# Hybrid encoder trunk: where the squares of the last tile are summed, and two pieces of ScalarE work moved

## The chip, the core and the metric

The kernel runs on one core of a Trainium2 chip. The metric is the device time of one execution in microseconds (us), the median of several runs; a profile is one such execution with the hardware profiler on. The engines are TensorE (PE; its weight loads are shown apart as PEld), VectorE (DVE), ScalarE (ACT), GpSimd (POOL) and SyncE (SP), which issues most loads.

## The reference

Two layers over 512 tokens of 1024 channels. `rms` divides each token by the root of its mean square and multiplies by a gain.

```python
for l in range(2):
    h = (silu(rms(x) @ w_gate) * (rms(x) @ w_up)) @ w_out      # 1024 -> 2 x 2816 -> 1024
    x = x + 0.5 * rms(h)
    h = rms(x) @ mix_w_in                                      # DeltaNet heads | convolution channels
    o = concat(gated_delta_rule(h), silu(layer_norm(causal_conv31(glu(h)))))
    x = x + rms(o @ mix_w_out)
    h = (silu(rms(x) @ w_gate2) * (rms(x) @ w_up2)) @ w_out2
    x = rms(x + 0.5 * rms(h))
```

In the gated delta rule the tokens are in chunks (the kernel takes four of 128), a state is carried from chunk to chunk, and the output `o` of each head is divided by the root of its mean square.

## The kernel before

Channels lie on the partitions (8 tiles of 128 for `x`), tokens on the free axis. Each large product is made of three products of rounded parts: high weight by high input, high by low, low by high (`tile`, lines 656 to 660). ScalarE makes the high part of a weight slot (`high`, line 1365), VectorE the low part (`weight_low`, line 2099). The engines run in parallel, each through its own instructions in the order in which they are written, and are held together by semaphores that count; nothing plans the order but this text.

**Stages and hand-overs.** Each layer has an FFN, a mixer and an FFN. Behind each stage but the very last, its output `y` (8 tiles) is normalised and added to `x`, and the next stage's inputs `xh` and `xl` are made: a hand-over, five in all (three behind an FFN, two behind a mixer). For this the sum of `y`'s squares over all channels is needed. ScalarE squares each tile from its bank into `sqr` (`y_square`); VectorE adds tiles 0 to 6 into `acc` (`y_sum`, line 2109, semaphore `ysum`). The last tile is made in two token halves of 256. When the first half is done (`y_half`), ScalarE squares it (line 1385, `ylast_sq`), VectorE adds it to `acc` (`y_sum_half`, line 2168, `ysum_part`), and TensorE sums over the channels with products by a column of ones (`token_sums`, line 665: one per chunk of 128 tokens, each shown as two records). ScalarE takes the root (line 1388), VectorE the reciprocal, TensorE spreads it over the partitions (`spread_first`, line 689), VectorE updates `x` (lines 2149, 2150), ScalarE makes `xh` (line 1406), VectorE `xl` (line 2160), and TensorE starts the next stage with half the tokens of three input tiles (lines 748, 750, 755). Meanwhile TensorE makes the second half of the last tile: in an FFN the last 8 of 22 steps (`k0` to `k0 + 7`), in the mixer 8 steps (`mix_last`). The second half's squares go the same way inside the next stage's first products, in `next_inputs` on VectorE and in `y_second_sums` on TensorE.

**First Strassen pairs.** The 16 middle gate/up pairs of each of the four FFNs are Strassen forms (`body`). ScalarE makes from a gate weight a negated copy (line 1503), to which GpSimd's accumulating DMA adds the weight (line 606, `form_added`), and the high part (line 1504), twice, one half at a time. In the first body ScalarE does the silu of the last plain pair (`silu(SP0 - 1, 0)`, line 1487) and then `first_forms(1, 0)`. VectorE waits for this silu in `pair(4, ...)` and goes on with the form sums (lines 2288 to 2290), the low parts (2314, 2298) and `up_second` (line 2321), which raises `c22_out`. TensorE's product `p4` of the pair before waits for `c22_out` (line 903); it is the third of the products of the second body.

**The scan.** For each of four chunks `c` ScalarE scales the state (line 1935), copies the new values `vn` (line 1938) and the keys (line 1924), and squares the chunk's output (`o_square(c)`, line 1905), which waits for `on` from VectorE (line 2773). TensorE's products that read `vn` are at lines 1256 and 1260, those that give it at line 1241.

Of the kernel before, what the change touches and what calls it, by code (L numbers as in the profile page):

```python
# [19 lines left out]
ALU = mybir.AluOpType  # L20
# [26 lines left out]
def trunk_kernel(nc, x, ffn1_norm_pre, ffn1_w_in, ffn1_w_out, ffn1_norm_post, mix_norm_pre, mix_w_in,  # L47
# [11 lines left out]
    KD = D // P  # L59
# [195 lines left out]
    with ctx:  # L255
# [28 lines left out]
        def sem(name):  # L284
# [21 lines left out]
        ylast_sq = sem("ylast_sq")  # L306
        y_half, ysum_part, ssq_part, root_part, col_part, bc_part, x_part, xh_part, xs_part = [
            sem(n) for n in ("y_half", "ysum_part", "ssq_part", "root_part", "col_part", "bc_part", "x_part",
                             "xh_part", "xs_part")]
# [310 lines left out]
        def _(pe):  # L620
# [50 lines left out]
            def x_sums(stage, l):  # L671
# [4 lines left out]
                else:  # L676
                    token_sums(acc[:]).then_inc(ssq_full, 1)

            def y_first_sums(stage, l):
                pe.wait_ge(ysum_part, (3 * l + stage) * 2 + 1)  # L680
                token_sums(acc[:], chunks=HALVES[0]).then_inc(ssq_part, 1)

            def y_second_sums(hand):
                pe.wait_ge(ysum_part, hand * 2 + 2)
                token_sums(acc[:], chunks=HALVES[1]).then_inc(ssq_full, 1)

# [32 lines left out]
            def first_units(u0, stage, stat_q, l):  # L719
# [40 lines left out]
                if stage or l:  # L760
                    for n in range(3):
                        pe.wait_ge(lo_full, l * UNITS + (u0 + n + 1 + SLOTS))
                    for k in range(HALVED):
                        pe.wait_ge(xh_part, hand * HALVED + k + 1)
                        high_products(k, tokens_of(0))
                        if k == 1:
                            spread_second(before, bl)
                        pe.wait_ge(xs_part, hand * HALVED + k + 1)
                        low_products(k, tokens_of(0))
                        if k == 0:  # L770
                            y_second_sums(hand)
                    for k in range(KD):
                        tokens = tokens_of(1) if k < HALVED else slice(0, T)
                        pe.wait_ge(xh_ready, l * NXS + stage * KD + k + 1)
                        high_products(k, tokens)
                        pe.wait_ge(xs_ready, l * NXS + stage * KD + k + 1)
                        low_products(k, tokens)
# [96 lines left out]
            def ffn(f, l):  # L874
# [80 lines left out]
                for m in range(KD):  # L955
                    pe.wait_ge(y_done, l * NY + (m + YB + stage * KD - 3))
                    for part, (k0, nk) in enumerate(OUT_PARTS):
# [8 lines left out]
                        for k in range(k0, k0 + nk):  # L966
# [4 lines left out]
                            if m < KD - 1:  # L971
                                mm = tile(in_bank(y_bank(m, stage, l)), n % SLOTS, k - k0, hh[:, k, :], hl[:, k, :],
                                          k == 0, k == KF - 1)
                            else:
                                mm = half_tile(k, 0)
                                if part < 2:
                                    mm = half_tile(k, 1)
                        if m == KD - 1 and part == 2:
                            mm.then_inc(y_half, 1)
                            for k in range(k0, k0 + nk):  # L980
                                if k == k0 + 3:
                                    y_first_sums(stage, l)
                                if k == k0 + 5:
                                    spread_first(stage, l)
                                mm = half_tile(k, 1)
                        mm.then_inc(unit_done, 1)

            for l in range(L):
# [309 lines left out]
                def mix_last(part):  # L1298
                    tokens = tokens_of(part)
                    for k in range(2 * CT):  # L1300
                        if part and k == 3:
                            y_first_sums(1, l)
# [57 lines left out]
        def _(act):  # L1360
# [93 lines left out]
            def ffn(f, l):  # L1454
# [104 lines left out]
                def body(s, odd, first=False, final=False, plain=None):  # L1559
# [3 lines left out]
                    first_part(s, odd)  # L1563
                    if first:
                        silu(SP0 - 1, 0)
                    if final:
                        act.wait_ge(prod_done, st * PRODS + 7 * s + 2)
                        high(u0 + 2 * (KF - 1), 2, 8, l)
                    else:
                        first_forms(s + 1, 1 - odd)  # L1570
                    if plain is not None and not odd:
                        act.wait_ge(conv_lo, plain + (st * NCONV + 1))
# [151 lines left out]
            for l in range(L):  # L1724
# [203 lines left out]
                for c in range(NC):  # L1928
# [12 lines left out]
                    if c == NC - 2:  # L1941
                        keys_out(c + 1)
                    if c == 0:
                        z_refill(0)
# [5 lines left out]
                    if c == 3:  # L1950
                        z_gate(1)

                        act.activation(warm[:], eps[:], ACT.Sqrt)
                    o_square(c)
                act.wait_ge(oss_ready, l * (H + 1) + H + 1)
# [95 lines left out]
        def _(dve):  # L2051
# [111 lines left out]

            def y_sum_half(part, stage, l):
                dve.wait_ge(ylast_sq, (3 * l + stage) * 2 + part + 1)
                dve.wait_ge(ysum, l * NYQ + (stage + 1) * (KD - 2))
                tokens = tokens_of(part)
                dve.tensor_tensor(acc[:, tokens], acc[:, tokens], sqr[:, (KD - 1) % 2, tokens],
                                  ALU.add).then_inc(ysum_part, 1)

            def row_first(stage, l):
                y_sum_half(0, stage, l)
                dve.wait_ge(root_part, 3 * l + stage + 1)
# [6 lines left out]
            def next_inputs(stage, gain, l):  # L2180
# [4 lines left out]
                low_half(0, 0, stage, gain, l)  # L2185
                y_sum_half(1, before, bl)
                update_half(2, 0, before, bl)
# [761 lines left out]
```

## Time and profile before

| | us |
|---|---|
| median of 3 runs (lowest, highest) | 1975.64 (1975.39, 1976.35) |
| the profiled execution | 1976.71 |
| its span | 1975.0 |

| engine | busy us | share of the span |
|---|---|---|
| PE | 1946.8 | 99% |
| PEld | 1746.6 | 88% |
| DVE | 1430.2 | 72% |
| ACT | 1161.8 | 59% |
| POOL | 149.4 | 8% |

TensorE's granted clock was 0.999 of full speed over the span. An engine's idle time counts only if another engine or the end waits for what comes behind it.

### The profile page before, as it was taken

What the parts mean: (1) busy time and instruction counts of PE and PEld (TensorE: products, weight loads), DVE (VectorE), ACT (ScalarE), POOL (GpSimd) and SP (SyncE); (2) the same over time, 40 slices, a digit from 0 to 9 for tenths busy, and PEclk for the clock granted to TensorE, in tenths of its full rate; (3) what the DMA queues carried; (4) which work ended last, traced back from release to release, by engine and by line L of the source; (5) the groups of instructions that cost most, each with busy time, mean ns of one, the idle gap of its engine ahead of it and who ended that gap; (6) DMA issues with size and microseconds to landing.
All of it is one profiled execution on the core that took longest, in us unless ns stands there. A gap on an engine that the chain in (4) does not pass through costs nothing.

```text
span 1975.0 us, 33173 instructions
## 1 busy us (share of the span) xinstructions
PE 1946.8 (99%) x12162; PEld 1746.6 (88%) x12162; DVE 1430.2 (72%) x2109; ACT 1161.8 (59%) x1957; POOL 149.4 (8%) x196
## 2 busy tenths in 40 slices
PE   9999999999999999999999999999999999999997
PEld 7999988878988899988889999888889888999886
DVE  5889832699885888872388888337998868888524
ACT  6576742457866667662266767325587656676513
POOL 1111000011000011100001110000110000111000
PEclk9999999999999999999999999999999999999999
DMA  6466533276222366643326664432761224666421
GB/s 177 116 153 155 144 110 102 68 170 147 65 54 86 86 150 159 156 127 96 102 65 138 156 155 121 116 103 75 171 141 45 61 78 114 153 158 148 150 96 43
DMA packets 351426, 232.52 MB, mean 118 GB/s; under 512 B 11122, under 2 KB 324948, under 8 KB 351316
## 3 DMA queue, kind: packets, MB, share of 16 engines
q1 hardware_dynamic: 327396, 177.55, 31.5%
q0 software_dynamic: 23904, 53.49, 15.0%
q8 instruction: 70, 1.15, 0.2%
q14 instruction: 40, 0.33, 0.0%
q10 hardware_dynamic: 16, 0.00, 0.0%
HBM read 175.43 MB, written 2.10 MB: 90 GB/s over the span
## 4 chain that ended last, share of the span: by engine, by line
PE 78%; DVE 15%; ACT 3%; issue 2%; DMA 1%; SPq 0%; POOL 0%; DVEq 0%; ACTq 0%
PE res L658 10%; PE res L660 9%; PE res L659 9%; PE res L893 8%; PE res L896 7%; PE res L895 7%; DVE u L2522 6%; PE sp L824 3%; PE sp L896 3%; PE sp L895 3%; PE sp L893 3%; PE res L824 2%; DVE cacc L2604 2%; PE sp L658 1%; PE res L755 1%
## 5 line engine op out<-in xcount | busy, mean ns | idle before, releaser
L2099 DVE TENSOR_TENSOR wl<-raw,wh 128x1024 fp32r<-128x1024 f32 (+1 forms) x167 | 197.3, 1185 | 335.2 <-ACT wh L1365 334.6
L1365 ACT ACTIVATE wh<-raw 128x1024 fp32r<-128x1024 f32 (+1 forms) x205 | 209.7, 1029 | 329.5 <-PE res L660 235.9
L893 PE MATMUL res<-xh,wh 128*128 128x256 f32 x768 | 218.1, 284 | 3.3 <-ACT wh L1523 1.7
L895 PE MATMUL res<-xl,wh 128*128 128x256 f32 x768 | 217.3, 283 | 0.0
L896 PE MATMUL res<-xh,wl 128*128 128x256 f32 x768 | 217.3, 283 | 0.0
L658 PE MATMUL res<-xh,wh 128*128 128x512 f32 x536 | 213.5, 398 | 2.1 <-DVE xl L2217 1.8
L660 PE MATMUL res<-xh,wl 128*128 128x512 f32 x536 | 208.9, 390 | 0.0
L659 PE MATMUL res<-xl,wh 128*128 128x512 f32 x536 | 208.9, 390 | 0.0
L660 PE MATMUL res<-hh,wl 128*128 128x512 f32 (+1 forms) x528 | 198.4, 376 | 0.0
L659 PE MATMUL res<-hl,wh 128*128 128x512 f32 (+1 forms) x528 | 198.4, 376 | 0.0
L658 PE MATMUL res<-hh,wh 128*128 128x512 f32 (+1 forms) x528 | 198.4, 376 | 0.0
L606 POOL DMA_DIRECT2D wl<-raw x128 | 109.0, 856 | 985.2 <-ACT wl L1503 972.7
L2522 DVE SCALAR_TENSOR_TENSOR u<-glu,call,u 128x512 f32<-128x512 f32 x240 | 167.8, 745 | 0.3
L893 PEld LDWEIGHTS res<-xh,wh 128*128 128x128 f32 x768 | 147.3, 192 | 4.9 <-ACT wh L1523 2.7
L895 PEld LDWEIGHTS res<-xl,wh 128*128 128x128 f32 x768 | 147.4, 192 | 0.2
L896 PEld LDWEIGHTS res<-xh,wl 128*128 128x128 f32 x768 | 147.4, 192 | 0.0
L893 PE MATMUL res<-th,wh 128*128 128x256 f32 x512 | 145.0, 283 | 1.3 <-ACT us L1542 1.3
L895 PE MATMUL res<-tl,wh 128*128 128x256 f32 x512 | 144.9, 283 | 0.0
L895 PE MATMUL sp<-tl,wh 128*128 128x256 f32 x512 | 144.9, 283 | 0.0
L896 PE MATMUL sp<-th,wl 128*128 128x256 f32 x512 | 144.9, 283 | 0.0
L893 PE MATMUL sp<-th,wh 128*128 128x256 f32 x512 | 144.9, 283 | 0.0
L896 PE MATMUL res<-th,wl 128*128 128x256 f32 x512 | 144.9, 283 | 0.0
(421 smaller groups left out, 4891.3 us busy)
## 6 DMA issues: line engine op xcount, KB each, us to landing
raw<-in_ffn_w_in SPq DMA_DIRECT2D x176, 512.0 KB, 4.0
wl<-raw POOLq DMA_DIRECT2D x128, 256.0 KB, 5.3
raw<-in_mix_w_in SPq DMA_DIRECT2D x48, 512.0 KB, 3.9
raw<-in_ffn_w_out SPq DMA_DIRECT2D x46, 512.0 KB, 3.9
raw<-in_ffn_w_out SPq DMA_DIRECT2D x48, 448.0 KB, 3.8
wl<-raw POOLq DMA_DIRECT2D x38, 512.0 KB, 4.6
raw<-in_mix_w_out SPq DMA_DIRECT2D x16, 512.0 KB, 4.0
xin<-in_x SPq DMA_DIRECT2D x8, 256.0 KB, 5.0
```

Of the source, the lines that this page charges most:

```text
L606: pool.dma_start(wl[:, 2, ks, :].bitcast(F32), raw[:, 2 * ((SP0 + s) % 2), ks, :], accum_op=ALU.add).then_inc(form_added[half], 16)
L658: pe.matmul(bank, wh[:, slot, j, :], hi, start=first, stop=False)
L659: pe.matmul(bank, wh[:, slot, j, :], lo, start=False, stop=False)
L660: return pe.matmul(bank, wl[:, slot, j, :], hi, start=False, stop=last)
L824: mm = pe.matmul(row_banks(c)[:, half, :], h[:, k, tokens], w[:, k % SLOTS, 4 * half:4 * half + 4, :].rearrange("p a b -> p (a b)"), start ...
L893: pe.matmul(bank, wh[:, slot, j, :], hi[:, k, :], start=first and k == 0, stop=False, skip_group_check=True)
L895: pe.matmul(bank, wh[:, slot, j, :], lo[:, k, :], start=False, stop=False, skip_group_check=True)
L896: mm = pe.matmul(bank, wl[:, slot, j, :], hi[:, k, :], start=False, stop=k == 3, skip_group_check=True)
L1365: act.activation(wh[:, slot, 0:nk, :], raw[:, slot, 0:nk, :], ACT.Copy).then_inc(hi_full, 1)
L2099: dve.tensor_tensor(wl[:, slot, 0:nk, :], raw[:, slot, 0:nk, :], wh[:, slot, 0:nk, :].bitcast(F32), ALU.subtract).then_inc(lo_full, 1)
L2522: ins = dve.scalar_tensor_tensor(u[:, t, :], src, w, u[:, t, :], ALU.mult, ALU.add)
L2604: ins = dve.scalar_tensor_tensor(cacc[:, n % 2, :], pre[:, k:k + T], w, cacc[:, n % 2, :], ALU.mult, ALU.add)
```

## The change

The first halves' and second halves' additions on VectorE (`y_sum_half`) are gone. TensorE sums `acc` (tiles 0 to 6, all four chunks) on its own in `y_other_sums` and then adds the last tile's squares straight from `sqr` into the same column sums. `y_other_sums` stands before step `k0 + 2` of the first half in an FFN and before step 6 in the mixer; the first half's sums stand one step earlier than before; the second half's stand between the high and the low products of input tile 0. `spread_first` and `spread_second` stay where they were. The silu in the first Strassen body follows `first_forms`. `o_square(c)` follows the copies of chunk `c + 1`, and the last stands behind the loop.

```diff
--- before.py
+++ after.py
@@ -304,8 +304,8 @@
         gate_scaled, pair_free, silu_done, h_ready = sem("gate_scaled"), sem("pair_free"), sem("silu_done"), sem("h_ready")
         y_done = sem("y_done")
         ylast_sq = sem("ylast_sq")
-        y_half, ysum_part, ssq_part, root_part, col_part, bc_part, x_part, xh_part, xs_part = [
-            sem(n) for n in ("y_half", "ysum_part", "ssq_part", "root_part", "col_part", "bc_part", "x_part",
+        y_half, ssq_part, root_part, col_part, bc_part, x_part, xh_part, xs_part = [
+            sem(n) for n in ("y_half", "ssq_part", "root_part", "col_part", "bc_part", "x_part",
                              "xh_part", "xs_part")]
         dve_step, pair_step = sem("dve_step"), sem("pair_step")
         mix_free = sem("mix_free")
@@ -676,13 +676,17 @@
                 else:
                     token_sums(acc[:]).then_inc(ssq_full, 1)
 
+            def y_other_sums(stage, l):
+                pe.wait_ge(ysum, l * NYQ + (stage + 1) * (KD - 2))
+                token_sums(acc[:], last=False)
+
             def y_first_sums(stage, l):
-                pe.wait_ge(ysum_part, (3 * l + stage) * 2 + 1)
-                token_sums(acc[:], chunks=HALVES[0]).then_inc(ssq_part, 1)
+                pe.wait_ge(ylast_sq, (3 * l + stage) * 2 + 1)
+                token_sums(sqr[:, (KD - 1) % 2, :], first=False, chunks=HALVES[0]).then_inc(ssq_part, 1)
 
             def y_second_sums(hand):
-                pe.wait_ge(ysum_part, hand * 2 + 2)
-                token_sums(acc[:], chunks=HALVES[1]).then_inc(ssq_full, 1)
+                pe.wait_ge(ylast_sq, hand * 2 + 2)
+                token_sums(sqr[:, (KD - 1) % 2, :], first=False, chunks=HALVES[1]).then_inc(ssq_full, 1)
 
             def spread_half(part):
                 for n, c in enumerate(HALVES[part]):
@@ -763,12 +767,12 @@
                     for k in range(HALVED):
                         pe.wait_ge(xh_part, hand * HALVED + k + 1)
                         high_products(k, tokens_of(0))
+                        if k == 0:
+                            y_second_sums(hand)
                         if k == 1:
                             spread_second(before, bl)
                         pe.wait_ge(xs_part, hand * HALVED + k + 1)
                         low_products(k, tokens_of(0))
-                        if k == 0:
-                            y_second_sums(hand)
                     for k in range(KD):
                         tokens = tokens_of(1) if k < HALVED else slice(0, T)
                         pe.wait_ge(xh_ready, l * NXS + stage * KD + k + 1)
@@ -972,13 +976,15 @@
                                 mm = tile(in_bank(y_bank(m, stage, l)), n % SLOTS, k - k0, hh[:, k, :], hl[:, k, :],
                                           k == 0, k == KF - 1)
                             else:
+                                if part == 2 and k == k0 + 2:
+                                    y_other_sums(stage, l)
                                 mm = half_tile(k, 0)
                                 if part < 2:
                                     mm = half_tile(k, 1)
                         if m == KD - 1 and part == 2:
                             mm.then_inc(y_half, 1)
                             for k in range(k0, k0 + nk):
-                                if k == k0 + 3:
+                                if k == k0 + 2:
                                     y_first_sums(stage, l)
                                 if k == k0 + 5:
                                     spread_first(stage, l)
@@ -1298,7 +1304,9 @@
                 def mix_last(part):
                     tokens = tokens_of(part)
                     for k in range(2 * CT):
-                        if part and k == 3:
+                        if not part and k == 6:
+                            y_other_sums(1, l)
+                        if part and k == 2:
                             y_first_sums(1, l)
                         if part and k == 5:
                             spread_first(1, l)
@@ -1561,13 +1569,13 @@
                     first_sum(s, odd, first)
                     act.sem_inc(hi_full, 2)
                     first_part(s, odd)
-                    if first:
-                        silu(SP0 - 1, 0)
                     if final:
                         act.wait_ge(prod_done, st * PRODS + 7 * s + 2)
                         high(u0 + 2 * (KF - 1), 2, 8, l)
                     else:
                         first_forms(s + 1, 1 - odd)
+                    if first:
+                        silu(SP0 - 1, 0)
                     if plain is not None and not odd:
                         act.wait_ge(conv_lo, plain + (st * NCONV + 1))
                     second_part(s, odd)
@@ -1940,6 +1948,8 @@
                         keys_out(c + 1)
                     if c == NC - 2:
                         keys_out(c + 1)
+                    if c:
+                        o_square(c - 1)
                     if c == 0:
                         z_refill(0)
                         act.wait_ge(o_full, l * NC + 1)
@@ -1951,7 +1961,7 @@
                         z_gate(1)
 
                         act.activation(warm[:], eps[:], ACT.Sqrt)
-                    o_square(c)
+                o_square(NC - 1)
                 act.wait_ge(oss_ready, l * (H + 1) + H + 1)
                 act.activation(gt["orr"][:, 0:16], gt["oss"][:, 16:32], ACT.Sqrt).then_inc(oroot, 1)
                 z_refill(2)
@@ -2161,15 +2171,7 @@
                                          xh[:, k, tokens].bitcast(F32), ALU.mult,
                                          ALU.subtract).then_inc(xs_ready if part else xs_part, 1)
 
-            def y_sum_half(part, stage, l):
-                dve.wait_ge(ylast_sq, (3 * l + stage) * 2 + part + 1)
-                dve.wait_ge(ysum, l * NYQ + (stage + 1) * (KD - 2))
-                tokens = tokens_of(part)
-                dve.tensor_tensor(acc[:, tokens], acc[:, tokens], sqr[:, (KD - 1) % 2, tokens],
-                                  ALU.add).then_inc(ysum_part, 1)
-
             def row_first(stage, l):
-                y_sum_half(0, stage, l)
                 dve.wait_ge(root_part, 3 * l + stage + 1)
                 dve.reciprocal(rcol[:, 0:2], rsq[:, 0:2]).then_inc(col_part, 1)
 
@@ -2183,7 +2185,6 @@
                 update_half(0, 0, before, bl)
                 update_half(1, 0, before, bl)
                 low_half(0, 0, stage, gain, l)
-                y_sum_half(1, before, bl)
                 update_half(2, 0, before, bl)
                 row_second(before, bl)
                 low_half(1, 0, stage, gain, l)
```

## Rows read from the trace of the kernel before

**Rows 1.** TensorE's waits: who was waited for, us in total, times, longest.

```profile
PE res L748 <- ACT xh L1406: 4.4, 10, 0.6
...
PE res L755 <- DVE xl L2160: 1.9, 5, 0.4
PE sp L1256 <- ACT vn L1938: 1.8, 2, 1.0
...
PE res L893 <- ACT wh L1523: 1.7, 2, 1.1
PE res L893 <- ACT us L1542: 1.3, 1, 1.3
PE res L893 <- ACT wh L1513: 1.1, 2, 0.6
```

**Rows 2.** Timeline of the first hand-over: start, length, engine, line, tiles, [idle before].

```profile
364.88 0.38 PE L689 MATMUL sp<-ident,rcol 128*128 128x128 f32 x2
...
367.54 0.28 PE L750 MATMUL res<-xh,wl 128*128 128x256 f32 x1
...
368.02 0.50 PE L665 MATMUL sp<-ones,acc 128*128 128x1 f32 x4
...
371.48 0.39 PE L748 MATMUL res<-xh,wh 128*128 128x256 f32 x1 [0.33 <-ACT xh L1406]
```

**Rows 3.** Timeline of TensorE around four chunks of token sums.

```profile
36.59 0.94 PE L665 MATMUL sp<-ones,acc 128*128 128x1 f32 x8
37.39 0.49 PE L658 MATMUL sp<-xh,wh 128*128 128x512 f32 x1
```

**Rows 4.** Timeline of the first mixer's last tile, first half: steps 0 and 6.

```profile
624.84 0.28 PE L658 MATMUL res<-hig,wh 128*128 128x256 f32 x1
...
627.00 0.28 PE L658 MATMUL res<-hic,wh 128*128 128x256 f32 x1
...
627.34 0.69 DVE L2109 TENSOR_TENSOR acc<-acc,sqr 128x512 f32<-128x512 f32 x1
```

**Rows 5.** Timeline of VectorE before the first hand-over: tile 6 of an FFN.

```profile
352.06 0.68 DVE L2109 TENSOR_TENSOR acc<-acc,sqr 128x512 f32<-128x512 f32 x1
```

**Rows 6.** Timelines of VectorE, TensorE and ScalarE in the first layer's scan.

```profile
560.00 0.68 DVE L2764 TENSOR_TENSOR St<-sd,sp 128x512 f32<-128x512 f32 x1
...
563.46 1.06 PE L1241 MATMUL sp<-St,Wy 128*128 128x128 f32 x8
...
564.02 0.31 ACT L1905 ACTIVATE osq<-on 128x128 f32<-128x128 f32 x1 [7.20 <-DVE on L2773]
...
567.00 1.16 PE L1256 MATMUL sp<-vn,kdec 128*128 128x128 f32 x8 [0.90 <-ACT vn L1938]
...
577.13 0.31 ACT L1905 ACTIVATE osq<-on 128x128 f32<-128x128 f32 x1 [0.89 <-DVE on L2773]
```

**Rows 7.** Timelines around the first Strassen pair of FFNs 1, 2 and 3.

```profile
78.91 0.41 DVE L2321 TENSOR_TENSOR us<-us,res 128x256 f32<-128x256 f32 x1
...
81.81 0.28 PE L893 MATMUL sp<-th,wh 128*128 128x256 f32 x1
...
693.20 0.63 ACT L1487 ACTIVATE gs<-gs 128x512 f32<-128x512 f32 x1 [0.37 <-DVE gs L2250]
...
695.30 0.61 ACT L1504 ACTIVATE wh<-raw 128x512 fp32r<-128x512 f32 x1
...
699.52 0.42 DVE L2321 TENSOR_TENSOR us<-us,res 128x256 f32<-128x256 f32 x1
...
701.15 0.28 PE L893 MATMUL sp<-th,wh 128*128 128x256 f32 x1
...
1050.96 0.63 ACT L1487 ACTIVATE gs<-gs 128x512 f32<-128x512 f32 x1 [2.09 <-DVE gs L2250]
...
1057.29 0.41 DVE L2321 TENSOR_TENSOR us<-us,res 128x256 f32<-128x256 f32 x1
...
1058.88 0.28 PE L893 MATMUL sp<-th,wh 128*128 128x256 f32 x1
```

## The prediction

> **What bounds the kernel now.** I read the table of busy times (above) first: TensorE is busy for 99% of the span, so the time is TensorE's instruction stream plus the few places where it waits. Then I read TensorE's list of waits [rows 1]. The reader is to see that the waits which this change can touch are small and counted: ten of 0.44 us on the first products of a stage (two at each of five hand-overs), two of 0.9 us in the scan on `vn`, and in the four FFNs single waits on what the first Strassen pairs need: 1.7 us in two, 1.3 in one, 1.1 in two. Then I read a hand-over in order of time [rows 2], the price of sums on TensorE [rows 3], the mixer's and the FFN's last tiles [rows 4, 5], the scan [rows 6] and the first Strassen pairs [rows 7]. What is added to TensorE's stream counts in full, and so does a wait that goes. Outside these places it does not wait for ScalarE or VectorE, so a shift there changes nothing.
>
> **The sums of squares, and where they cost.** A 256-column product follows the one before it in 0.12 us: the 18 products from 624.84 to 627.00 take 2.16 us [rows 4]. Four chunks of token sums are eight records, and the product behind them starts 0.80 us after their first [rows 3]; that product then takes 0.49 us instead of 0.39, 0.1 us for the start behind them. I take 0.88 us for four chunks. Two chunks are the x4 record group at 368.02 [rows 2]. Before, each hand-over had four chunks (two and two). After, it has eight: `y_other_sums` sums the accumulated squares alone, and the two halves of the last tile are summed as before, straight from `sqr`. So 0.88 us is added at each of 5 hand-overs, 4.4 us.
> These eight records stand in front of the product that raises `y_half`, so nothing hides them: everything behind `y_half` starts later by as much.
> The Trainium skill's page "TensorE: Matmul & The Clock Gate", section "Back-to-back issue gap", gives an isolated product N/2.4 + 2.5 ns, some 3 ns for a product of one column; by that the four chunks would cost nothing and the sum of this change would be 4.4 us lower. The same section says that in a stream the spacing is set by the weight load too. The row gives 0.10 us for each of the eight records, so it decides for the second statement.
>
> **The wait that comes with it.** `y_other_sums` needs the sum over tiles 0 to 6. In an FFN VectorE has done it early: tile 6's is at 352.06 [rows 5], some 8 us ahead of the place. In the mixer the last tile has only 8 steps a half, and the sums are put before step 6, which TensorE reaches at 627.00, while VectorE's last addition starts at 627.34 and takes 0.69 [rows 4], done at 628.03. TensorE stands in order, so its products wait 1.05 us. VectorE can't be earlier: the addition is behind a weight subtraction that waits for ScalarE. This is paid in 2 mixers: 2.1 us. Behind the waiting sums stand the last six products of the half, `y_half`, the Square, the root and the whole hand-over.
>
> **What the removed additions give.** First half: the sums of the squares may start when the Square is done, about 0.45 us sooner, and are moved from behind three steps to behind two (0.36 us). But `spread_first` stays before step 5, and TensorE reaches it at 364.88 in either order, having done the same sums and the same steps. VectorE and ScalarE have nothing else to do for the result. I take 0; at most it is the 0.36 us by which the sums move.
> Second half: the sums move ahead of the three low products, from 368.02 to 367.66 (0.12 behind the last high product at 367.54) [rows 2]. The root, the scaling of the last tile and `xh` of tile 2, which stand in order on ScalarE, move 0.36 us, and VectorE, rid of its addition (0.42 us), follows. TensorE's wait at 371.48 (0.33 us, with the slower start behind it) goes, and from there VectorE's additions and subtractions set the pace for two more steps, all 0.36 us earlier. So 0.36 us is won at each of 5: 1.8 us. The bounds are 0 and the two waits together, 0.33 and one of 0.4 on `xl`.
> Sum of this part: 4.4 + 2.1 - 1.8 = **+4.7 us**. TensorE does more, and the chain that was shortened was not the one that decided.
>
> **The scan's squares.** In iteration 2 ScalarE is held at `o_square(1)` for 7.20 us until VectorE gives `on` at 564.02, and has its four squares (0.31 us each, some 1.2 together), four scalings and the copy of `vn` still to do. What these need is there earlier: the state at 560.68 and TensorE's values at 564.52 [rows 6]. Squares last, `vn` is ready at about 565.1, and TensorE, which stood 0.90 us before 567.00, doesn't wait. The slower start behind a wait goes too (1.16 instead of 1.06 us). 1.0 us. VectorE's state update waits for the same products and moves along. What is late next is the last square: `o_square(3)` at 577.13 [rows 6] is now behind `o_square(2)`, a silu and a table load. ScalarE gets there at about 576.4, so it wins 0.75 where TensorE wins 1.0; the row of roots and the first turned head lie behind it and are nearly tight, which costs 0.15. I take -0.85 us a layer, **-1.7 us**, between 0 and -2.0.
>
> **The silu behind the second pair's weights.** The silu and the four copies behind it start 0.52 us apart: silu at 693.20, the fourth copy at 695.30 [rows 7]. With the silu last, ScalarE hands the first copy to the accumulating DMA 0.5 us earlier (and by its own idle wait for VectorE more), and TensorE's wait for this DMA shrinks. But the silu itself starts some 2 us later, and behind it VectorE is stuck in order: the product `hraw`, three form sums, two weight subtractions, then `up_second`, for which the product p4 of the first pair waits (`c22_out`). This gives four sums, in the order of the FFNs:
> First: `up_second` starts at 78.91, +2.0 and 0.41 long, done at 81.3; p4 stood at 81.81 and could be at 81.3 with its DMA wait 0.5 shorter: -0.4.
> Second: the silu waited 0.37 for `gs`, so it is 1.7 late; `up_second`, at 699.52 before, + 1.7 + 0.42 and 0.05 of signalling gives 701.7, while p4 was at 701.15: +0.55 and 0.08 of slower start, +0.6.
> Third: the silu waited 2.09 us for `gs` (1050.96) and held up the copies behind it, and thereby the copy that TensorE waited for (1.3 us in rows 1). It still runs at 1050.96, so VectorE loses nothing; p4 goes from 1058.88 to the end of `up_second`, 1057.29 + 0.41 and signalling: -1.05.
> Fourth: like the second, but it had a DMA wait of 0.56 us to lose: about +0.1.
> Sum -0.75, **-0.7 us**. Bounds: all of the four waits won, -3.1; the second's loss in each, +2.4.
>
> **The sum.** The profiled execution took 1976.71 us, its span 1975.0. With 4.7 - 1.7 - 0.7 = +2.3 us it is 1979.0. The median shown is 1.07 us lower, so the change gives 1977.9 against 1975.64. About 0.2% (4 us) is what can be told from no change.
>
> **Rivals.**
> (A) The late silu costs nothing, because p4 does not really wait for `up_second` or VectorE catches up. Then the four waits go whole, -3.1 instead of -0.7: 1975.5. For it: VectorE has idle time after `up_second` in the first pairs. Against: its row ends only 1.2 us before p4 in the second FFN.
> (B) The added records hide behind the running products: -4.4, 1973.5. Against it stands the row of eight.
> (C) Slower: ScalarE and not TensorE ends the scan. The moved `o_square(2)`, the silu and the table load stand before `o_square(3)`; if `vn` of chunk 3 comes less than 0.8 us earlier, the last root, the scaling of `on` and the first turned head are no earlier than before, or 0.3 later. It takes the whole 1.7 and 0.3 in each layer: +2.3, 1980.2, slower by 0.23%. It decides from the point where those 1.2 us of squares are more than ScalarE won.
>
> **Chances.** Forecast 0.62, A 0.15, B 0.06, C 0.13, others 0.04. The likeliest one's own range is 1976.5 to 1979.3; with A and C and the bounds of the silu the range is 1974.6 to 1980.2. Faster by over 0.2% (below 1971.7) needs B and A together: 0.03. Slower by over 0.2% (above 1979.6) is most of C and the upper edge of the forecast: 0.14. Same 0.83.
>
> **What would show it.** TensorE's busy time up by some 4 us. In both mixers a wait of about 1 us of the sums on VectorE's addition to `acc`, in no FFN. At the hand-overs the first wait on `xh` unchanged at 0.54, the second gone or small. No wait on `vn`. In the second and fourth FFN a new wait, at p4 of the first pair, on VectorE's `us`; the third's 1.3 us gone. I would be wrong if the mixers show no wait on `acc`, if the first wait on `xh` shrinks too, or if p4 starts without one.

## The result, and the profile after

| | before | after |
|---|---|---|
| median of 5 runs (lowest, highest) | 1975.64 (1975.17, 1976.98) | 1984.59 (1982.18, 1987.12) |
| profiled execution, its span | 1976.71, 1975.0 | 1982.39, 1980.7 |
| mean granted clock of the profiled execution | 0.999 | 0.997 |

The changed kernel is slower by 0.43%: the ratio is 1.0043, with the interval 1.0032 to 1.0054. I had said 1977.9 and a range up to 1980.2; it is 6.7 us above the one and 4.4 above the other.

TensorE's list of waits in the changed kernel, to be held against [rows 1] (who was waited for: us in total, times, longest):

```profile
PE res L897 <- DMA wl<-raw: 4.4, 5, 1.5
PE res L752 <- ACT xh L1414: 2.8, 5, 0.6
...
PE sp L665 <- DVE acc L2119: 1.8, 2, 0.9
...
PE sp L897 <- DVE us L2322: 0.6, 1, 0.6
...
PE sp L665 <- DVE usum L2743: 0.3, 1, 0.3
```

Three lines are as forecast. The waits on `xh` are 5 and not 10. The wait on `acc` is there, twice, 0.92 us each. The one on `vn` (1.8 us) is gone. The first line is the surprise: 4.4 us of waits on the accumulating DMA, where [rows 1] has 4.1 us on ScalarE's `wh` and `us` (and the kernel before one of 0.5 us on this DMA).

Three timelines of the changed kernel (start, length, engine, line, tiles, [idle before]). First TensorE at the first hand-over, to be held against [rows 2]:

```profile
366.19 0.36 PE L752 MATMUL res<-xh,wh 128*128 128x256 f32 x1 [0.54 <-ACT xh L1414]
...
366.98 0.50 PE L665 MATMUL sp<-ones,sqr 128*128 128x1 f32 x4
367.34 0.60 PE L759 MATMUL res<-xl,wh 128*128 128x256 f32 x3
...
370.45 0.39 PE L752 MATMUL res<-xh,wh 128*128 128x256 f32 x1
```

The first wait keeps its 0.54 us. The second sums stand ahead of the three low products, and the 0.33 us in front of the product that was at 371.48 have gone. Then the first mixer, against [rows 4]:

```profile
625.09 0.28 PE L660 MATMUL res<-hic,wl 128*128 128x256 f32 x1
626.29 1.05 PE L665 MATMUL sp<-ones,acc 128*128 128x1 f32 x8 [0.92 <-DVE acc L2119]
627.21 0.36 PE L658 MATMUL res<-hic,wh 128*128 128x256 f32 x1
...
625.55 0.68 DVE L2119 TENSOR_TENSOR acc<-acc,sqr 128x512 f32<-128x512 f32 x1
```

From the last product to the next one are 2.12 us where there were 0.12: the wait, the eight records, and the start behind them. And the scan, against [rows 6]:

```profile
563.44 0.60 ACT L1946 ACTIVATE vn<-sp 128x512 f32<-128x512 f32 x1 [2.47 <-PE sp L1247]
...
564.41 0.31 ACT L1913 ACTIVATE osq<-on 128x128 f32<-128x128 f32 x1
...
564.83 1.05 PE L1262 MATMUL sp<-vn,kdec 128*128 128x128 f32 x8
...
575.36 0.31 ACT L1913 ACTIVATE osq<-on 128x128 f32<-128x128 f32 x1 [0.23 <-DVE on L2774]
```

ScalarE makes `vn` before the four squares, and TensorE's products on it start without a wait.

**Where the 5.7 us of span went.** I matched TensorE's instructions of the two traces one by one and took the shift between them in front of and behind each place; a step is the difference, with the slower start behind a wait in it:

| place | predicted | in the trace |
|---|---|---|
| three hand-overs behind an FFN | 3 x 0.52 | 3 x 0.42 (+0.79, then -0.37) |
| two behind a mixer | 2 x 1.57 | 1.71 each, and 1.3 more in layer 2 |
| scan, both layers | -1.7 | -0.70 and -1.10 |
| first Strassen pairs, FFN 1 to 4 | -0.4, +0.6, -1.05, +0.1 | 0, +0.67, -0.18, +0.15 |
| later Strassen pairs | 0 | +1.2 (-0.7 at 222, +1.0 at 728, +0.4 at 1078, -0.6 at 1190, +1.15 at 1818) |
| start of the kernel | 0 | -0.7 |
| behind TensorE's last product, and drift | 0 | +0.3 |

Two of these are not the change's doing. The start is 0.7 us earlier in this execution and not at all in a second one of the same kernel (number 10). And of the step at 1190, some 0.8 us stand at 1197, where ten of the eleven profiles taken after the kernel before gain 0.45 to 0.8 us on its profile, whatever the edit.

The 1.3 us more in layer 2 stand in the granted clock. Stretches of the changed kernel (busy us of PE, PEld, DVE, ACT, POOL with counts, then the clock, the DMA share and GB/s):

```profile
1604.00:1608.00 4.00, 3.08 (x26) 2.88 (x26) 1.83 (x2) 1.49 (x3) 0.00 (x0) 1.00 0.25 68
1608.00:1612.00 4.00, 4.00 (x24) 4.00 (x23) 0.17 (x1) 2.29 (x4) 0.00 (x0) 0.58 0.21 63
1612.00:1616.00 4.00, 3.46 (x29) 3.28 (x28) 3.30 (x9) 2.12 (x6) 0.00 (x0) 0.99 0.02 4
```

And the same place of the kernel before:

```profile
1608.00:1612.00 4.00, 3.46 (x29) 3.14 (x27) 3.41 (x10) 2.26 (x6) 0.00 (x0) 1.00 0.00 1
```

TensorE waited 0.92 us on `acc` and did eight records of one column at 1606. Behind 1608.6 it then ran at half its clock (1.2 instead of 2.4 GHz) for 3.4 us, by the mean of 0.58 over 4 us (0.42 x 4 / 0.5), though it was busy all the time. The profile before shows no such fall until TensorE is done. This execution, with one fall, has a mean clock of 0.997. The 0.995 and 0.996 of three of the five runs say that others had more, and that the number differs between executions.

**What the accumulating DMAs did.** Issues on GpSimd in the second FFN's first pairs, with their time to landing. Before (the first line of each pair is the issue, with its start at the end; the second is from issue to landing):

```profile
L606 POOL DMA_DIRECT2D wl<-raw x1: 857/857/857, 694.6 to 694.6; - x1
DMA to landing us min/median/max: 3.3/3.3/3.3
...
L606 POOL DMA_DIRECT2D wl<-raw x1: 843/843/843, 695.7 to 695.7; - x1
DMA to landing us min/median/max: 3.8/3.8/3.8
```

After:

```profile
L606 POOL DMA_DIRECT2D wl<-raw x1: 857/857/857, 693.6 to 693.6; - x1
DMA to landing us min/median/max: 4.0/4.0/4.0
...
L606 POOL DMA_DIRECT2D wl<-raw x1: 841/841/841, 694.8 to 694.8; - x1
DMA to landing us min/median/max: 5.3/5.3/5.3
```

They are issued 1.0 and 0.9 us sooner, and take 0.7 and 1.5 us longer. The second one lands at 700.1 and not at 699.5, and TensorE waits for it. SyncE's queue and TensorE in the changed kernel show what it runs beside and what that costs:

```profile
692.82 0.38 SPq L504 DMA_DIRECT2D raw<-in_ffn_w_in  x1
...
700.18 0.36 PE L897 MATMUL res<-xh,wh 128*128 128x256 f32 x1 [0.59 <-DMA wl<-raw]
```

### The profile page after: what moved, and what is told of

Its sections match the earlier page's. It is cut to its first block, busy times and chain, and to the rows that moved or that the text cites. A ratio compares the mean times of both kernels' runs of the same rounds, so it can differ in the third digit from the quotient of the medians.

```text
span 1980.7 us, 33233 instructions
## 1 busy us (share of the span) xinstructions
PE 1952.5 (99%) x12202; PEld 1752.8 (88%) x12202; DVE 1425.7 (72%) x2099; ACT 1161.1 (59%) x1957; POOL 149.8 (8%) x196
## 4 chain that ended last, share of the span: by engine, by line
PE 80%; DVE 13%; issue 3%; ACT 2%; DMA 2%; POOL 0%; SPq 0%; DVEq 0%; ACTq 0%; POOLq 0%
PE res L658 10%; PE res L659 10%; PE res L660 10%; PE res L897 7%; PE res L900 7%; PE res L899 7%; DVE u L2523 5%; PE sp L828 3%; PE sp L897 3%; PE sp L900 3%; PE sp L899 3%; PE res L828 2%; DVE cacc L2605 2%; PE sp L658 1%; DMA wl<-raw 1%
```

## The experiments

Each was timed beside the kernel before on the same chip, with 5 to 11 runs. The kernel before gave 1976.83, 1976.13 and 1976.48 us (medians of 27, 33 and 14 runs) in the three groups: numbers 1, 2, 3 and 5; 4, 6, 7 and 8; 9 and 10. Steps are those of the shift against the profile of the kernel before, by the same matching.

**1. The sums alone.**

```diff
+def y_other_sums(stage, l):
+    pe.wait_ge(ysum, l * NYQ + (stage + 1) * (KD - 2))
+    token_sums(acc[:], last=False)
-    pe.wait_ge(ysum_part, (3 * l + stage) * 2 + 1)        # y_first_sums, y_second_sums alike
-    token_sums(acc[:], chunks=HALVES[0]).then_inc(ssq_part, 1)
+    pe.wait_ge(ylast_sq, (3 * l + stage) * 2 + 1)
+    token_sums(sqr[:, (KD - 1) % 2, :], first=False, chunks=HALVES[0]).then_inc(ssq_part, 1)
...
```

> The kernel before with the part on the sums of squares alone (acc summed by TensorE, sqr straight into the same columns). Theory (stream, wait and clock): the three hand-overs behind an FFN cost 0.36 us each, the two behind a mixer 1.8 us each by the eight records and the 0.9 us wait, and 1.3 us more for each mixer hand-over in which TensorE's granted clock falls to 1.2 GHz behind that wait: +4.7 us without a fall, up to +7.3 with two, and a spread between runs. Rival (the loops): most of the 9 us of the whole change comes from the silu's accumulating DMAs landing later; then this kernel is no more than 4.7 us above before in every run and the clock stays up in the mixers.

Measured: 1984.49 us (1983.24 to 1986.86), ratio 1.0045 (1.0031 to 1.0059). The sums are about the whole loss; the +7.7 us between the medians is a little over the +7.3 that I had expected at most. At the five hand-overs the steps add up to +4.7 us, as forecast. The rest is +0.7 in a loop of the second FFN at 728 (experiment 9), +0.35 in the first scan, where VectorE is late with `usum`, smaller steps of both signs, and one fall of the clock:

```profile
1020.00:1024.00 4.00, 4.00 (x12) 3.17 (x11) 1.97 (x6) 4.00 (x8) 0.00 (x0) 0.57 0.44 133
```

It cost 1.6 us. It stands behind the layer boundary's sixteen one-column records at 1018, which the kernel before has too, and not in a mixer.

**2. The silu alone.**

```diff
 first_part(s, odd)
-if first:
-    silu(SP0 - 1, 0)
...
     first_forms(s + 1, 1 - odd)
+if first:
+    silu(SP0 - 1, 0)
```

> The kernel before with the silu behind the second pair's weights alone. My prediction had -0.7 us. The trace of the changed kernel says +0.5 us in the first pairs, because the accumulating DMAs, issued 1 us sooner, land up to 2.4 us after their issue later than before beside the load of the gate weight. Theory: +0.5 us, with a wait of TensorE on an accumulating DMA in the second and third FFN. Rival: the shift also changes later DMA waits in the loops, +2 us or more.

Measured: 1975.4 us (1974.36 to 1979.4), ratio 0.9998 (0.9989 to 1.0007): nothing that can be told. Steps in the first pairs: +0.1 in the first FFN, +0.67 in the second, -0.43 in the third (1.5 and 0.3 won, 1.4 given back) and +0.15 in the fourth, together the +0.5 that I had expected. TensorE in this kernel:

```profile
701.29 0.36 PE L893 MATMUL sp<-th,wh 128*128 128x256 f32 x1 [0.64 <-DVE us L2321]
...
1057.07 0.36 PE L893 MATMUL res<-xh,wh 128*128 128x256 f32 x1 [1.30 <-DMA wl<-raw]
```

The first row is p4's late wait, 0.64 us where I had +0.6. The second is the wait that I had taken as won in the third FFN; it has only moved from the copy to the DMA behind it.

**3. The scan alone.**

```diff
+    if c:
+        o_square(c - 1)
...
-    o_square(c)
+o_square(NC - 1)
```

> The kernel before with the scan's squares moved back alone. Theory: -1.8 us, no wait of TensorE on vn, the clock as before. Rival: the wait comes back at the end of the scan (last root, first turned head), 0 to -0.5 us.

Measured: 1974.15 us (1972.12 to 1976.04), ratio 0.9985 (0.9976 to 0.9994). The steps are -1.04 and -1.07 us. This part is worth what was forecast, and a little more. In the whole change the first layer gets only 0.70, because a wait of 0.28 us on `usum` comes up behind (the last line of the list of waits above). It comes with the sums and not with this edit: number 1 loses 0.35 us at this place with the scan as it was. The clock did fall once in this profile, 12.4 us from the start and so far ahead of the scan; it hides the gain in the two spans (1974.3 and 1975.0 us).

**4. The changed kernel, but the mixer's sums of the accumulated squares in the second half.**

```diff
-if not part and k == 6:
+if part and k == 1:
     y_other_sums(1, l)
```

> The changed kernel with the mixer's y_other_sums behind y_half, before step 1 of the last tile's second half, where VectorE's sum is done. Theory: each mixer wins the 0.9 to 1.05 us wait and with it its own risk of a clock fall (1.3 us); the eight records still cost 0.8 us each. 2.1 us below the changed kernel without a fall, 2.1 to 3.5 in the median. Rival (the place does not matter, the records and the longer chain do): 0 to -0.5 us.

Measured: 1979.78 us (1976.89 to 1982.91), ratio 1.0017 (1.0008 to 1.0026). TensorE here:

```profile
629.05 1.05 PE L665 MATMUL sp<-ones,acc 128*128 128x1 f32 x8
630.40 0.50 PE L665 MATMUL sp<-ones,sqr 128*128 128x1 f32 x4
```

No wait on `acc`. A mixer's hand-over costs 0.41 and 0.42 us, not 1.71: 2.6 us less in the two. The ratios say 3 to 5 us (1.0033 and 1.0043 against 1.0017), with intervals of 2 us to each side. So at a mixer the place before step 6 was the dear thing (1.2 us, number 5), and the records the smaller one (0.87 us, number 9).

**5. The wait alone, without records.**

```diff
 for k in range(2 * CT):
+    if not part and k == 6:
+        pe.wait_ge(ysum, l * NYQ + 2 * (KD - 2))
```

> The kernel before, and in the mixer's last tile TensorE waits before step 6 of the first half for VectorE's sum of tiles 0 to 6; no product is added or moved. Theory (the wait lets the clock fall): +2.1 us for two waits of 1.05 us, and in some runs 1.3 us more a mixer, with a granted clock of half within some us behind the wait. Rival (the one-column products, not the wait, let it fall): +2.1 us in every run and the clock stays up.

Measured: 1979.29 us (1976.75 to 1982.21), ratio 1.0014 (1.0005 to 1.0023). The steps are +1.18 us each, so 2.4 us are the two waits themselves; the medians are 2.5 us apart. TensorE at the first, and the one fall of the clock:

```profile
627.23 0.39 PE L658 MATMUL res<-hic,wh 128*128 128x256 f32 x1 [0.92 <-DVE acc L2111]
```
```profile
1016.00:1020.00 4.00, 4.00 (x19) 3.43 (x19) 2.01 (x7) 3.56 (x8) 0.00 (x0) 0.63 0.47 135
```

The fall is again at the layer boundary, beside the sixteen records and not behind the two waits, so this profile does not show what I had expected of the clock.

**6. The gains without the records:** the scan, and the second sums between the high and low products, with VectorE's addition kept.

```diff
     high_products(k, tokens_of(0))
+    if k == 0:
+        y_second_sums(hand)
...
     low_products(k, tokens_of(0))
-    if k == 0:
-        y_second_sums(hand)
```

> The kernel before with the scan's squares moved back, and with the second half's column sums between the high and the low products of tile 0, VectorE's addition kept. No product is added. Theory: -1.8 us for the scan and -0.3 us at each of 5 hand-overs (the sums move from 368.02 to about 367.74, when the addition is done): -3.3 us. Rival (the second half was won by the addition that VectorE no longer did): the hand-overs give nothing, -1.8 us.

Measured: 1974.37 us (1972.21 to 1976.55), ratio 0.9990 (0.9981 to 0.9999). Each hand-over gains 0.15 to 0.21 us, where I had expected 0.3. TensorE at the first:

```profile
368.50 0.61 PE L665 MATMUL sp<-ones,acc 128*128 128x1 f32 x4
372.08 0.39 PE L748 MATMUL res<-xh,wh 128*128 128x256 f32 x1 [0.16 <-ACT xh L1406]
```

So of the 0.37 us that the change wins in a second half, about half comes from moving the sums ahead of three products, and the other half, some 0.2 us, from VectorE's addition that is gone. That needs no extra record.

**7. Number 6, and in the third FFN the silu between the two halves of the second pair's forms.**

```diff
     for half in range(2):
+        if half and between:
+            between()
...
-    if first:
+    if first and not two:
         silu(SP0 - 1, 0)
...
-    first_forms(s + 1, 1 - odd)
+    first_forms(s + 1, 1 - odd, between=(lambda: silu(SP0 - 1, 0)) if first and two else None)
```

> The kernel e6_best, and in the third FFN alone the silu stands between the two halves of the second pair's first forms. Theory: the first accumulating DMA starts 2.6 us sooner, the second where it stood, the wait of 1.32 us on us shrinks to about 0.3: 1.0 to 1.2 us below e6_best. Rival (what the DMAs win is lost again at the second product): 0 to -0.3 us.

Measured: 1972.72 us (1971.18 to 1975.62), ratio 0.9983 (0.9974 to 0.9993). It has the lowest median of all, 0.17% below the kernel before; the interval overlaps that of number 6. The third FFN gains 1.07 + 0.31 - 0.57 = 0.8 us, less than the 1.0 to 1.2 expected. TensorE there:

```profile
1051.69 0.35 PE L893 MATMUL res<-th,wh 128*128 128x256 f32 x1 [0.26 <-ACT us L1544]
1055.25 0.35 PE L893 MATMUL res<-xh,wh 128*128 128x256 f32 x1 [0.46 <-ACT wh L1525]
```

The wait of 1.3 us is down to 0.26. One of 0.46 on `wh` comes behind it (the 0.57 that is given back), none on a DMA.

**8. Number 2, with SyncE's next gate weight held until the second pair's accumulations have landed.**

```diff
+for each in form_added:
+    sp.wait_ge(each, st * 16 * NS + 32)
 with sp.Fori(0, (NS - 2) // 2) as i:
```

> The kernel before with the silu moved behind the second pair's weights, and SyncE's first load in each FFN's Strassen part held until both accumulating DMAs of the second pair have landed. Theory (the accumulating DMAs are slow because that load is under way): they land 3.3 to 3.8 us after their issue in all four FFNs, instead of 4.0 to 6.2, and the first pair's waits on them go; the held load may cost elsewhere. Rival (their length has another cause): 4 to 6 us as before.

Measured: 1979.49 us (1976.58 to 1981.0), ratio 1.0013 (1.0003 to 1.0023). The accumulations of the second FFN, the first with its issue:

```profile
L608 POOL DMA_DIRECT2D wl<-raw x1: 857/857/857, 695.2 to 695.2; - x1
DMA to landing us min/median/max: 3.3/3.3/3.3
...
L608 POOL DMA_DIRECT2D wl<-raw x1: 843/843/843, 696.4 to 696.4; - x1
DMA to landing us min/median/max: 3.7/3.7/3.7
```

With no load beside them they land in 3.3 and 3.7 us (4.0 and 5.3 in the changed kernel); the other FFNs have 3.3 to 4.2. With the load gone the steps in the first pairs are -0.37, +0.67, -1.02 and +0.15 us, where the prediction had -0.4, +0.6, -1.05 and +0.1. So the load beside the accumulations is what made the step on the silu fail, in the first and the third FFN. And TensorE's wait on the late `up_second` now stands in all four:

```profile
PE sp L895 <- DVE us L2323: 2.8, 4, 0.7
```

The kernel is slower all the same, since the held load pushes later ones together: accumulations take 6.0 to 6.6 us in the next loop pairs, with steps of +1.2 and +1.4 us at 708 and 1066.

**9. The kernel before with eight records more at the two places, which read `ones` and wait for nothing.** Their sums go to spare columns and are not read.

```diff
+def eight_records():
+    for c in range(NC):
+        pe.matmul(stat[:, 40 + c:41 + c], ones[:], ones[:, 0:1], start=True, stop=True, ...)
```

> The kernel before with eight one-column records (products of a matrix of ones, into columns that nobody reads) before step k0 + 2 of the last tile's first half in the FFNs and before step 6 in the mixers; no wait, and the rest as before. Theory: each stands in the stream with 0.8 us and nothing hides it: 5 x 0.8 = +4.0 us. It also shows whether the longer landing of the accumulating DMAs in the second FFN's loop (+1 us near 728 us in every kernel with the sums) comes with added records. Rival (the records overlap with the products around them): under +2 us.

Measured: 1981.37 us (1980.39 to 1983.94), ratio 1.0029 (1.0019 to 1.0039). The steps at the five places are +0.88, +0.87, +0.87, +0.90 and +0.87 us, 4.4 in all, and the clock doesn't fall in its profile. TensorE at the first mixer:

```profile
627.11 0.95 PE L681 MATMUL sp<-ones 128*128 128x1 f32 x8
627.92 0.36 PE L658 MATMUL res<-hic,wh 128*128 128x256 f32 x1
```

0.10 us for each record, hidden behind nothing, and 0.07 for the slower start behind eight: rival B is out. It also shows +0.8 us at 728, with the records alone. The two accumulations before it are issued 0.35 us ahead of SyncE's load and 1.3 behind it, in the kernel before, in number 5 and here, yet they land after 5.2 and 6.5, 5.4 and 6.1, and 6.9 and 7.4 us.

The traces show one thing more that differs there. The queue that loads the engines' instructions moves one packet of 16 KB, which takes 0.95 us, at 727.21 here and at 728.18 in the kernel before. Queues in this kernel between the issue and the landing of the first accumulation, 723.4 to 730.2 (packets, MB, share of the 16 engines):

```profile
q0 software_dynamic: 279, 0.51, 40.9%
q8 instruction: 1, 0.02, 0.9%
```

In the kernel before there is none between its issue and its landing, 722.4 to 727.5. So it is in all twelve profiles: in the five of kernels with added records this packet comes 3.8 to 4.1 us behind the first issue, and the accumulation takes 6.8 to 7.0 us; in the other seven it comes 5.4 to 5.8 us behind, as or after the accumulation has landed (5.1 to 5.4 us). At 222, in the first FFN, the same five have the packet 0.4 to 0.9 us earlier than the other seven and a landing of 6.3 to 6.5 us instead of 6.8 to 7.2, and TensorE gains 0.6 to 0.7 us. No added record has run by then, so a later stream can't be the reason; number 8, whose stream is 3.5 us late at 728, also has the short landing of 5.1 us. What the five share is products that were added to TensorE's instructions. No run moves the instruction packet alone, so that it is the cause is likely and not shown.

**10. The changed kernel again.** No edit.

> The changed kernel once more, beside the kernel before on the same chip. Theory: +6 us for the steps that its trace shows and up to 3 us more for clock falls, +6 to +9 in the median; in its profile the wait on acc in both mixers, and a fall of the clock at one of: a mixer's hand-over, the sums at 1018 us, the first products at 12 us. Rival (the first measurement was a bad draw): within +5 us.

Measured: 1983.4 us (1981.73 to 1985.4), ratio 1.0033 (1.0021 to 1.0045). Its profile (span 1983.7, mean clock 0.996) has falls in other places than the first one:

```profile
628.00:632.00 4.00, 4.00 (x23) 4.00 (x23) 0.17 (x1) 2.30 (x4) 0.00 (x0) 0.57 0.36 109
1060.00:1064.00 4.00, 2.49 (x12) 2.52 (x13) 2.84 (x4) 1.78 (x4) 0.86 (x1) 0.70 0.74 178
```
```profile
1061.51 0.50 PE L897 MATMUL res<-xh,wh 128*128 128x256 f32 x1 [1.96 <-DMA wl<-raw]
```

Now the clock falls behind the wait on `acc` in the first mixer, and beside the 1.96 us on the DMA in the third FFN. A third fall begins at 1611, behind the same wait in the second mixer. In the first trace the first two places had no fall; the second mixer has one in both.

## Why the prediction was wrong

The part on the sums was right in size, the scan too. Three steps failed.

**The clock was held for constant.** I set the sum against the profiled execution and took off 1.07 us "lower"; that holds only if both kernels lose as much in granted clock. They don't. Runs in groups of the mean granted clock (mean us, count):

| clock | before | changed kernel (5 runs) | before | number 10 |
|---|---|---|---|---|
| 0.995 | | 1986.4 (2) | | 1984.7 (1) |
| 0.996 | | 1984.6 (1) | 1978.0 (1) | 1984.5 (2) |
| 0.997 | 1978.6 (7) | 1982.3 (2) | 1976.9 (4) | 1982.6 (2) |
| 0.998 | 1976.4 (18) | | 1976.0 (7) | 1981.7 (1) |
| 0.999 | 1974.6 (2) | | 1974.8 (2) | |

Beside the changed kernel's first five runs stand those of before of the first group of experiments. In the last two columns, which shared a chip, the kernels differ by 5.7 us at 0.997 and at 0.998. The 5.7 us between the spans of the two profiles is the same figure by chance: it has a fall of 1.3 us in it, and the profiled execution before took 1976.71 us at 0.999, where seven others at 0.999 took 1974.2 to 1974.8. By the equal clocks, the rest of the loss of the medians (1.2 us for number 10; 3.3 for the first five runs, of 8.95) goes with a lower clock; for the first five this is a reckoning, since the clocks of the runs of before that stood beside them are not on record.

The clock's mean is 0.9978 for before, and 0.9960 and 0.9965 for the changed kernel. A fall of some 3.4 us at half clock is 0.0009 of the mean, so that is one to two falls more an execution, at the 1.3 to 1.6 us each that single falls cost (the changed kernel, number 1). Which edit brings them is not settled. The wait alone has 0.9974, the sums alone 0.9974, the records 0.9982, the silu 0.9983, the scan 0.9980, and with single runs rounded to 0.001 these are hardly apart. The version that was fastest has 0.9973.

The twelve profiles have ten falls of 3.4 us: three at 12 to 13 us (numbers 3, 4 and 8), three at the layer boundary, 1015 to 1020 (numbers 1, 5 and 7), three at a mixer's last tile and one at 1061 (the changed kernel's two profiles); before, 2, 6 and 9 have none. The start and the boundary are the same in every kernel. The falls in the mixers are the ones that go with the change: three in the eight places where TensorE waited on `acc` (two each in the changed kernel's two profiles and in 1 and 5), none in the sixteen without that wait. That points at the wait and not at the records, on few cases. The Trainium skill's page "TensorE: Matmul & The Clock Gate" (its first part, on the clock gate) has the two levels too, and ties them to how busy TensorE has been; the rows agree in that the falls of the changed kernel's two profiles stand behind a wait of 0.9 to 2 us, but the same wait has no fall in the other execution.

**The silu** (forecast -0.7, trace +0.6). The step that failed is "TensorE's wait for this DMA shrinks". I moved the issue of the accumulating DMA and kept its length. Issued 1 us sooner, in the third FFN 2.7 and 2.6 us sooner, it runs beside SyncE's gate weight for longer and lands no sooner (5.3 for 3.8 us in the second FFN, 6.2 for 3.8 in the third). That cost the forecast gains of the first and the third FFN; number 8, without that load, has them. In the second and fourth `up_second` set the time, and +0.67 and +0.15 stand against +0.6 and +0.1. The other half, VectorE's lateness, was right almost to the row: `up_second` at 701.17, and p4 waits for it in the fourth FFN of the changed kernel, in the second of number 2, and in all four of number 8. Rival A is out: the late silu is not free.

**The later Strassen pairs** (forecast 0, trace +1.2). "Outside these places it does not wait for ScalarE or VectorE, so a shift there changes nothing" left out the DMAs. +0.7 to +1.0 us at 728 and +0.4 to +0.6 at 1078 come in every kernel with records added (the changed kernel, 1, 4, 9 and 10) and in none without. The DMAs at 728 got longer; number 9 has the likely cause, a load of instructions that falls inside them, and it is not shown.

**What was right.** Records: 4.4 forecast, 4.4 measured by themselves (number 9). The wait in the mixers: 1.05 forecast, 0.92 in the row, 1.2 with the slower start (number 5). The second half's -0.36 is -0.37, the first half's 0 is 0, and the first wait on `xh` is unchanged. All five hand-overs: +4.7 forecast, +4.7 without the fall. Scan: -1.7 forecast, -1.8 in the whole and -2.1 by itself. Rival C, ScalarE ending the scan, is out. TensorE's busy time rose from 1946.8 to 1952.5 us; 4 of these are the records, the rest mostly the fall of the clock. Of what the Trainium skill's page "TensorE: Matmul & The Clock Gate" says in its section "Back-to-back issue gap", the rule on the spacing of a stream decides, as row and experiment have it, and the one of an isolated product doesn't: 0.10 us a record and not 3 ns. The prediction took that 3 ns from the section's formula alone; the table in the same section has some 60 cycles, about 25 ns, for 1 to 64 columns, and this too is a quarter of what was measured.

So of the 5.7 us in the spans, 2.3 were in my sum. The other 3.4 are the silu (+1.3 against my term), the later pairs (+1.2), one fall of the clock (+1.3), and -0.4 of the start, the end and the scan. Some of that is luck of the one execution: the start and the step at 1197 took 1.5 us off, which the change does not give.

## What to carry to other kernels

Where TensorE is busy for 99% of the span, work moved to it from an idle engine is paid in full, however small its shape: here 0.10 us for each one-column record, against a VectorE addition that cost the path some 0.2 us. When an edit issues a DMA sooner, look at what else is on the queues at the new time before you count the gain: here the DMA took longer by as much as it was issued sooner, and its reader waited for its landing all the same. Put the place of a new wait where its data are early (experiment 4: three steps later, and 1.3 us twice are gone), and time such a change over several executions, since two profiles of one kernel can differ by 3 us.

## What I had not expected of the hardware

- The granted clock falls to half for about 3.4 us in the middle of dense work, at places that differ between executions of the same kernel: 1608 in one profile of the changed kernel, 628, 1061 and 1611 in the other. The one at 1608 cost 1.3 us, the one at 1020 in number 1 cost 1.6. The kernel before has them as well, by its mean clock of 0.9978 against 0.999 in a profile without one.
- At the start, TensorE waited 2.35 to 2.64 us on VectorE ahead of its first large products in the three profiles whose clock fell at 12 to 13 us, and 1.99 us or less in the other nine, where it did not.
- An accumulating DMA of half a weight slot lands in 3.3 to 3.9 us with no load beside it (number 8, FFN 2 to 4), in 3.3 and 3.8 when it is issued 1.8 and 2.8 us behind SyncE's load (before), and in 6.2 when it is issued 0.2 us behind it (the changed kernel's third FFN). In the loop at 723 it takes 5.1 to 5.4 us in seven profiles and 6.8 to 7.0 in five, with issue times that are the same to 0.01 us relative to TensorE's stream; the five are those in which 16 KB of instructions are loaded while it is under way.
